# All eight gate/up k tiles in rounded and remainder parts, with a GpSimd subtraction, and four raw down-weight buffers

## What is computed

```python
def _swiglu(x, wg, wu, wd):
    return (jax.nn.silu(x @ wg) * (x @ wu)) @ wd

def run_block(args):
    xblk, e = args
    return _swiglu(xblk, w_gate[e], w_up[e], w_down[e])

yb = lax.map(run_block, (xb, block_e)).reshape(p, d)
yb = yb * buf_w[:, None].astype(yb.dtype)
return jax.ops.segment_sum(yb, buf_tok, num_segments=n + 1)[:n]
```

## Time and profile before

| | us |
|---|---|
| median of 3 runs | 1226.64 (1225.98 to 1227.47) |
| the profiled execution | 1225.67 |
| its span, first to last instruction | 1223.5 |
| PE busy | 1106.1 (90%) |
| DVE busy | 903.4 (74%) |
| ACT busy | 642.7 (53%) |
| POOL busy | 181.9 (15%) |

### The profile page before, as it was taken

The page is one execution under the profiler, slowest core; times in us unless marked ns, Lnnn a source line. Parts: engine busy times, 40 slices in busy tenths (PEclk is TensorE's granted clock), DMA queues, the critical chain, the costliest instruction groups (busy, mean ns, idle before and its releaser), DMA issues.

```text
span 1223.5 us, 18540 instructions
## 1 busy us (share of the span) xinstructions
PE 1106.1 (90%) x6014; PEld 811.6 (66%) x6014; DVE 903.4 (74%) x1333; ACT 642.7 (53%) x770; POOL 181.9 (15%) x185
## 2 busy tenths in 40 slices
PE   5999999999989999799999999999999999999700
PEld 3899999865444454467777777777777777777500
DVE  4422443365956777579899999989989888888878
ACT  4332221332421233257787777777777777777501
POOL 1000000000110110112222222222222222221102
PEclk9999999998879999899999999999999999999855
DMA  9542221436974143689999999999999999998996
GB/s 341 188 133 80 80 80 40 157 98 202 315 276 132 44 138 120 235 325 381 380 388 391 391 384 385 387 387 381 373 381 383 373 381 379 375 375 314 352 360 210
DMA packets 86545, 339.34 MB, mean 277 GB/s; under 512 B 12561, under 2 KB 36129, under 8 KB 59122
## 3 DMA queue, kind: packets, MB, share of 16 engines
q1 hardware_dynamic: 70130, 301.16, 67.2%
q0 software_dynamic: 16384, 37.78, 8.8%
HBM read 317.00 MB, written 42.86 MB: 294 GB/s over the span
## 4 chain that ended last, share of the span: by engine, by line
PE 46%; DMA 32%; DVE 14%; ACT 6%; issue 2%; SPq 1%; DVEq 0%; POOL 0%; POOLq 0%; ACTq 0%
DMA arena<-in_w_exp_down 28%; PE ps L1828 11%; DVE down_lo L1648 4%; PE ps L2259 4%; PE ps L2067 4%; ACT down_hi L1120 4%; PE ps L2238 3%; PE ps L2239 3%; PE ps L2240 3%; PE ps L1821 2%; PE ps L2242 1%; PE ps L2105 1%; PE ps L2226 1%; DMA arena<-expert_rows 1%; PE ps L2140 1%
## 5 line engine op out<-in xcount | busy, mean ns | idle before, releaser
L1653 DVE TENSOR_TENSOR gu_lo<-w_gu,gu_hi 128x2048 fp32r<-128x2048 f32 (+1 forms) x128 | 258.7, 2022 | 6.4 <-ACT gu_hi L1114 1.1
L1114 ACT ACTIVATE gu_hi<-w_gu 128x2048 fp32r<-128x2048 f32 (+1 forms) x128 | 217.9, 1703 | 0.0
L1648 DVE TENSOR_TENSOR down_lo<-arena,down_hi 128x2048 fp32r<-128x2048 f32 x64 | 146.7, 2293 | 58.0 <-ACT down_hi L1120 58.0
L2238 PE MATMUL ps<-gu_hi,xT_hi 128*112 128x512 f32 x448 | 182.8, 408 | 3.3 <-DVE xT_lo L1658 2.2
L2239 PE MATMUL ps<-gu_lo,xT_hi 128*112 128x512 f32 x448 | 177.9, 397 | 0.0
L2240 PE MATMUL ps<-gu_hi,xT_lo 128*112 128x512 f32 x448 | 177.3, 396 | 0.0
L1120 ACT ACTIVATE down_hi<-arena 128x2048 fp32r<-128x2048 f32 x64 | 122.7, 1918 | 64.0 <-DMA arena<-in_w_exp_down 56.1
L814 POOL DMA_INDIRECT expert_rows<-arena,row_idx x64 | 69.1, 1079 | 356.2 <-ACT arena L1159 340.1
L2259 PE MATMUL ps<-down_hi,actT_hi 128*112 128x512 f32 x256 | 106.6, 416 | 5.5 <-DVE actT_lo L1643 5.5
L807 POOL DMA_INDIRECT arena<-h_rows,token_idx x64 | 80.6, 1259 | 203.1 <-PE ps L2226 156.1
L1828 PE MATMUL ps<-w_hi,hT_hi 128*128 128x300 f32 x352 | 105.6, 300 | 1.4 <-DVE w_lo L1231 1.4
(11 more groups left out here) (310 smaller groups left out, 1989.8 us busy)
## 6 DMA issues: line engine op xcount, KB each, us to landing
w_gu<-in_w_exp_gate SPq DMA_DIRECT2D x64, 1024.0 KB
w_gu<-in_w_exp_up SPq DMA_DIRECT2D x64, 1024.0 KB
arena<-in_w_exp_down SPq DMA_DIRECT2D x64, 1024.0 KB
arena<-in_w_ada SPq DMA_DIRECT2D x16, 1024.0 KB, 6.9
arena<-in_w_in SPq DMA_DIRECT2D x12, 1200.0 KB, 5.6
arena<-expert_rows SPq DMA_DIRECT2D x9, 1024.0 KB, 13.4
arena<-in_w_ada_first SPq DMA_DIRECT2D x4, 2048.0 KB, 16.2
arena<-expert_rows SPq DMA_DIRECT2D x4, 2048.0 KB, 13.0
```

The costliest lines, as they stand in the source:

```text
L1114: a.activation(gu_hi[b % RING][:, :, ks], w_gu[b % U][:, :, ks], ACT.Copy).then_inc(s_ghi, 1)
L1648: v.tensor_tensor(down_lo[:, :, :], w_dn[b % RING], down_hi[:, :, :].bitcast(F32), ALU.subtract).then_inc(s_dlo, 1)
L1653: v.tensor_tensor(gu_lo[b % U][:, :, ks], w_gu[b % U][:, :, ks], gu_hi[b % RING][:, :, ks].bitcast(F32), ALU.subtract).then_inc(s_glo, 1)
L2238: pe.matmul(out, x_hi, gu_hi[r][:, :, k], start=(k == 0), stop=False)
```

## The change

All eight k tiles get rounded and remainder parts (SPLIT = 8), so the plain float32 product, `x_raw` and its ACT copy are gone. ACT's second part of `gu_hi` and `xT_hi`, and DVE's `xT_lo`, grow by one k tile; DVE's `gu_lo` stays at seven tiles (LOW_PARTS), and the eighth is subtracted by POOL (`last_k_low`). There are four raw down buffers; two of them lie in two separate pieces of 1024 columns each. SP fills buffers 2 and 3 before the loop and then loads the down weights of block j+4, not j+2. Nine small loads of modulation rows (`bcg2`) move from ahead of the loop to the end, and three other regions move to make room.

```diff
-SPLIT = 7
+SPLIT = 8
 PARTS = ((0, 4), (4, SPLIT))
+LOW_PARTS = ((0, 4), (4, SPLIT - 1))
...
-        w_dn = [region(a + W_COLS[0], FK, D) for a in RING_AT]
+        w_dn = [region(a + W_COLS[0], FK, D) for a in RING_AT] + [apart(PROJ0 + 4 * D, PROJ0 + 9 * D), apart(*DN3)]
...
                 if wait:
-                    sp.wait_ge(s_dlo, j - RING + 1)
+                    sp.wait_ge(s_dlo, j - U + 1)
...
             load_gate_up(3, 3, False)
-            sp.dma_start(bcg2[0].rearrange("p (c n) -> p c n", n=512), mod_row[1, 0:1, 2:4].broadcast_to([P, 2, 512])).then_inc(s_bcg, 16)
-            for b in range(SB):
-                sp.dma_start(bcg2[1][b * SS:(b + 1) * SS].rearrange("p (c n) -> p c n", n=512),
-                             mod_row[1, 1 + b:2 + b, 2:4].broadcast_to([SS, 2, 512])).then_inc(s_bcg, 16)
+            load_down(2, 2, False)
+            load_down(3, 3, False)
...
                     load_gate_up(i * U + (U + b), b, True)
-                    load_down(i * U + (b + RING), (b + RING) % U, True)
+                    load_down(i * U + (U + b), b, True)
...
+            def last_k_low(j, b):
+                g.wait_ge(s_ghi, j * 2 + 2)
+                g.tensor_tensor(gu_lo[b % U][:, :, SPLIT - 1], w_gu[b % U][:, :, SPLIT - 1], gu_hi[b % RING][:, :, SPLIT - 1].bitcast(F32),
+                                ALU.subtract).then_inc(s_gat, 1)
...
                         gather(i * U + (b + GATHER_AHEAD), (b + GATHER_AHEAD) % U)
+                    if not is_last or b + 2 < U:
+                        last_k_low(i * U + (b + 2), b + 2)
...
-                a.activation(x_raw[:, b % 2], xT_ps[:, SPLIT:KT], ACT.Copy).then_inc(s_xth, 1)
...
                     for k in range(*PARTS[part]):
+                        if k == SPLIT - 1:
+                            pe.wait_ge(s_gat, j + 2)
...
-                        pe.matmul(out, x_lo, gu_hi[r][:, :, k], start=False, stop=False)
-                for k in range(SPLIT, KT):
-                    o = pe.matmul(out, x_raw[:, b % 2, k - SPLIT], w_gu[q][:, :, k], start=False, stop=(k == KT - 1))
+                        o = pe.matmul(out, x_lo, gu_hi[r][:, :, k], start=False, stop=(k == KT - 1))
```

More of the change, by code:

```diff
@@ L106 @@
 W_COLS = (2 * KT * FF, FK * D)
+GU_HI0, GU_HI1 = WORK0 + W_COLS[0] + W_COLS[1], HT0 + D // 2
+assert GU_HI0 + 2 * KT * FF == WORK0 + 10 * D and GU_HI1 + 2 * KT * FF <= ST0
 def _constants():
@@ L202, in hybrid_step @@
         actT_lo = over_arena("actT_lo", MOD0 + 2 * FK * D + 2 * FK * T, [P, 2, FK, T])
[L203 removed]
+        gu_hi = [over_arena(f"gu_hi{n}", at, [P, 2, SPLIT, FF]) for n, at in enumerate((GU_HI0, GU_HI1))]
         gu_lo = [over_arena(f"gu_lo{n}", at, [P, 2, KT, FF]) for n, at in enumerate(GU_AT)]
@@ L332, in hybrid_step, with apart @@
         rowf = small(5, P, rows=1)
-        tab = region(_consts["before"][0] + P, 4, P, rows=1).bitcast(I32)
+        tab = region(TAB0, 4, P, rows=1).bitcast(I32)
         act_rows = region(MOD0 + 2 * FK * D + 4 * FK * T, 2, FF)
         silu_g = region(MOD0 + 2 * FK * D + 4 * FK * T + 2 * FF, 2, FF)
-        w_dn = [region(a + W_COLS[0], FK, D) for a in RING_AT]
+        def apart(first, second):
+            return arena[:, first:first + 2 * (second - first)].rearrange("p (k n) -> p k n", k=FK)[:, :, 0:D]
+        DN3 = (ARENA_W - 2 * (ARENA_W - WORK0 - 10 * D), WORK0 + 10 * D)
+        w_dn = [region(a + W_COLS[0], FK, D) for a in RING_AT] + [apart(PROJ0 + 4 * D, PROJ0 + 9 * D), apart(*DN3)]
+        assert DN3[0] >= HB0 + 2 * D and DN3[0] + D <= WORK0 and DN3[1] + D == GU_HI1
         x_rows = region(HB0, 2, D)
@@ L469, in hybrid_step @@
         s_wgu = [sem(f"w_gate_up_in{b}") for b in range(U)]
-        s_wdn = [sem(f"w_down_in{r}") for r in range(RING)]
+        s_wdn = [sem(f"w_down_in{r}") for r in range(RING)] + [s_cond, s_const]
+        WDN_BASE = (0, 0, 32, 32)
         s_dhi = sem("w_down_high_ready")
@@ L734, in _ @@
                 rank_rows(ranks_low[t], 0, 4, t)
-            load_down(last * U + 3, 3, True)
             for t in range(2, NT):
@@ L741, in _ @@
                 rank_rows(ranks_low[t], 0, 4, t)
+                if t == 2:
+                    for b in range(SB):
+                        sp.dma_start(bcg2[1][b * SS:(b + 1) * SS].rearrange("p (c n) -> p c n", n=512),
+                                     mod_row[1, 1 + b:2 + b, 2:4].broadcast_to([SS, 2, 512])).then_inc(s_bcg, 16)
             sp.wait_ge(s_gu, last * U + 4)
+            sp.wait_ge(s_dlo, last * U + 3)
             for rows, buf in kept(N, shared):
@@ L745, in _ @@
             sp.wait_ge(s_free, last * U + 4)
-            sp.wait_ge(s_dlo, last * U + 3)
             for t in LAST_ORDER:
@@ L823, in _ @@
             g.wait_ge(s_tab, 1)
-            for j in range(GATHER_AHEAD):
-                gather(j, j, j >= 2)
+            for j in range(2):
+                gather(j, j, False)
+            last_k_low(0, 0)
+            gather(2, 2)
+            gather(3, 3)
+            last_k_low(1, 1)
             def turn(i, is_last, is_first=False):
```

42 lines of the change are left out of this document (20 added, 22 removed).

## The result

The changed kernel takes 1237.9 us in the median of six runs (1233.4 to 1240.5), the kernel before 1226.3 us in six runs beside it. The ratio is 1.0101, 95% interval 1.0077 to 1.0125. The forecast was 1227 us and a range up to 1234 us. That execution is the slowest of the six: these two lie 14.9 us apart, the medians 11.6.

What follows compares the result with a forecast made beforehand. PE and DMA were taken as full together, DVE close behind. 62 x (9.88 - 9.86) = 1.2 us longer and 0.9 us shorter put 1225.67 at 1226.0 us, plus 1.0 us to the median: 1227 us, range 1214 to 1234 us.

Steps and rivals of the forecast that it cites:

- The end: After the loop: one 1.05 MB load leaves, 0.79 MB in nine small loads comes in between rank rows, costing zero.
- PE, 0.15 us a step shorter: Loop, PE: the 0.86 us float32 product goes, three single-pass products (0.71 us) come; step 9.63 us, 9.3 us over 62 steps.
- Four down buffers give back 4.8 us: Loop: down loads get two more steps, so the wait for late down loads goes, worth 4.8 us if the data comes.
- ACT and `xT_lo` cost nothing: Loop: ACT ends about 0.4 us later ahead of a waiting `down_hi`; DVE's `xT_lo` grows 0.14 us, hidden by idle time.
- DVE's reserve of 0.84 us: Loop: DVE's idle time per block in the kernel before, said to hide the longer `xT_lo`.
- GpSimd's subtraction, t = 1.15 us, and the two hold each other up: Loop: POOL's eighth-tile subtraction takes t, 1.15 us, and it and DVE's `gu_lo` delay each other by that whole length.
- 9.30 + t/2: Loop: lower bound in us on one step from the two-step ACT and DVE chain, t being POOL's subtraction time; 9.88 us.
- The step of 9.88 us, loop 603 us: Loop: forecast step against 9.86 us before; silu of block 1 to silu of block 62 takes 603 us.
- main case: Whole kernel: POOL and DVE hold each other up, PE waits for `xT_lo`; 1227 us, chance 0.48.
- Rival 1: Loop: POOL and DVE run side by side, DMA gives back 5.7 of 14.1 us; gain 9.3 us, 1217 us; chance 0.27.
- 0.9 us gained at `down_hi` of block 63: Last block: with its down load there before, `down_hi` waits only for PE and 0.9 us is gained.
- The signs: Expected in the profile: float32 product and `down_hi` load waits gone, PE waiting for `xT_lo`, `gu_lo` longer or later, step 9.88 us.

Runs made afterwards that it cites:

- e1: Changed kernel without its eight small loads of sample modulation rows in the end (sample rows get a wrong gate row): end 76.2 us, against 90.9.
- e12: Changed kernel with the eight loads replaced in place by one 0.5 MB load of the prompt's row, 128 partitions, 2 KB packets: ratio 1.0098 to the kernel before.
- e13: Changed kernel with the eight loads replaced in place by one 0.5 MB load of different DRAM rows, 2 KB packets: end 86.8 us, ratio 1.0063.
- e14: Changed kernel with the eight loads replaced in place by one 0.5 MB load of 128 whole rows, 4 KB packets: end 83.3 us, ratio 1.0056.
- e15: Changed kernel with one more SyncE wait: the fourth read of `expert_rows` is issued only once the eight loads have landed; end 81.2 us.
- e6: Changed kernel with down loads inside the loop cut to one of two k tiles (wrong outputs): loop 614.8 us, end 76.3 us.
- e7: Kernel of e2 with down loads inside the loop cut to one of two k tiles: loop 594.6 us.
- e3: Changed kernel with two raw down buffers instead of four, both late down loads back in the end: loop 602.7 us, end 90.4 us.
- e11: Kernel before, with the eight sample-row loads issued again between the third and fourth read of `expert_rows`: median 1236.5 us, slower by 0.96%.
- e2: Changed kernel without GpSimd's subtraction and PE's wait for it, PE reading the rounded last k tile instead: loop 604.6 us, first ten steps 9.64 us.
- e4: Changed kernel with the eighth k tile's remainder also made by VectorE, GpSimd doing none: loop 601.1 us, first ten steps 9.61 us.
- e9: Changed kernel with the eight sample-row loads issued behind the last read of `expert_rows`: time equal to the kernel before.
- e5: Changed kernel with the same sample rows at the same place brought by two loads of 64 partitions instead of eight: end 89.4 us.
- e10: Changed kernel with the load placing of e9 and the all-VectorE remainders of e4: 0.2% below the kernel before, interval to 1.0001.
- e8: Kernel before with down loads inside the loop cut to one of two k tiles: loop 601.0 us, against 601.4.

## Why the prediction was wrong, step by step

**The failed step is "The end": the 0.79 MB in nine small loads "issued between rank rows that are not yet due: zero".** The end is 13.7 us longer than before, and without the eight loads 14.7 us shorter than that (90.9 and 76.2, e1). The step counted bytes and due times. But a load is there only when its last part is, and the parts can drift apart.

What the runs show: wherever the fifth read had a spread of 1.0 us or less, the end took 75.6 to 81.2 us; wherever it had 3.3 us or more, 83.3 to 90.9 us, in 17 traces without exception. Where the fourth read had come with a spread of 4.1 us or less, the fifth was in step again; from 4.6 us on it never was, nor any later read. The fifth is issued only after an addition, about when the fourth lands, which gives laggards a pause to catch up in: from 1158 to 1160 us the DMA share is 0.62 in e1, and 1.03 in the changed kernel. That this is how step is regained is argued from these traces, and e15 shows that a pause does it. The loop hands over engines that are 0.6 to 4.6 us apart (third read), and one more load between the third and the fourth read, whichever it is (e12 to e14), takes them past what the pause can mend.

That lost step makes packets slow is shown as far as two things go. In e15 one wait is added, nothing less is moved, and the spread and the slow packets are both gone; but the wait also leaves fewer loads in the queue at once. In e6 and e7 the end's list of loads is that of the changed kernel, the eight included, the reads stay in step, and packets take 190 ns. Why packets take longer when the parts are out of step was not tried.

Why e6 and e7 kept in step isn't tested either. Their third reads had spreads of 0.7 and 1.0 us, but so had those of e3 and e11 (0.8, 1.0), which lost it. What differs is the queue: in e6 and e7 the fourth read was issued only 1.6 and 2.7 us before the last part of the third landed, in the changed kernel, e3 and e11 6.5 to 6.9 us before. So it stood in a queue that had nearly run dry, which fits e15.

**PE, 0.15 us a step shorter.** Right: the first ten steps of e2 are 9.64 us for 9.63 predicted.

**Four down buffers give back 4.8 us.** Wrong, it is nothing (e3). `down_hi`'s wait for loads did go; since the step was set by DVE's chain and by the transfers, it was worth nothing. The prediction read the late steps of before (9.96 us in the last 21) as the price of two buffers, but with four they are the same, 9.96.

**ACT and `xT_lo` cost nothing.** ACT: right. DVE's reserve of 0.84 us is used up by the subtraction.

**GpSimd's subtraction, t = 1.15 us, and the two hold each other up.** Right in kind: t is 1.27 and 1.29 us in the rows above, and `gu_lo` is longer by what it had to wait; where DVE goes first, `down_low` is held up in its place, as foretold. The rule of the Trainium skill (SBUF — State Buffer, "Who interferes with whom") that the two exclude each other agrees with the trace, except that the wait shows inside the later instruction's row. PE waits for `xT_lo` as foretold, 0.18 us in the block shown and 2.9 us in the 30 blocks from 700 to 1000 us. By 9.30 + t/2 the step would be 9.94 us; it is 9.84 in the unbroken stretches and 602.5/61 = 9.88 over the loop. The formula lets `gu_lo` begin t later; in the rows it is delayed by 0.84 and 1.06 us only, the rest of POOL's operation having passed before DVE is ready. Half of that on 9.30 us gives 9.72 to 9.83 us.

**The step of 9.88 us, loop 603 us.** It is 602.5 us, but half of this is luck. The prediction took DMA as full and not as a bound in its main case. e2 and e4 have no hold-up and gain nothing: the transfers stand at the same pace. Two bounds lay on each other, 9.84 us from the engines and 9.85 to 9.91 from the transfers (601.1 and 604.6 us by 61), and the prediction named one. Rival 1 (side by side, DMA gives back 5.7 of 14.1 us) undersized it as well: DMA gives back everything.

**0.9 us gained at `down_hi` of block 63.** Right, but small beside the rest: `down_hi` starts when PE is done, at 1150.43 us, and the additions begin 7.6 us behind silu of block 63, before 8.3 us: 0.7 us gained.

**The signs.** Those of the loop came as written. None was given for the end, since nothing was expected to happen there.

## What to carry to other kernels

A load moved into a stretch where the queue is never empty is not costed by its bytes: look at where the queue runs dry now, because that is where the DMA engines fall back into step, and put what is not urgent behind the last urgent read (e9) or wait for it (e15). GB/s well under its usual value at a full DMA share is the sign. And where two resources are full in the same window, don't credit a gain to relieving one: without the hold-up alone (e2, e4) or with fewer bytes alone (e6) the loop was no more than 1.4 us shorter, and only both together (e7) made it 8 us shorter.

## What the runs showed of the hardware

- The median 4 KB packet of before's whole trace took 159 ns. In the end the mean was 187 to 193 ns with the reads in step and 194 to 235 ns out of step, at the same DMA share: 14 to 17% of the packets took over 250 ns in step, 18 to 31% out of step.
- Even in step, the stretch in which the 64-row tile is read runs at about half speed (197 to 233 GB/s in e1 from 1160 to 1165 us, where 414 to 426 stand before and behind). The fifth read, 1 MB for 64 partitions, landed 4.9 us behind the fourth, which is 2 MB for 128 partitions and landed 6.2 us behind the third (last parts).
- One of the 16 parts of a load lags far behind the others in the loop: from 700 to 1000 us the spread of a down load is 14 to 17 us (median) in the changed kernel, e1, e2, e4, e5, e9, e10 and e12 to e15, which have four down buffers, 8 to 10 us in before, e3 and e11, which have two, and 1 us in e6 to e8, whose loads are cut. With deeper buffers the other parts run further ahead of the last one, and a load still counts from its last part; that would explain why depth gave no time, but no run tests it.
- A DVE subtraction that finds GpSimd's subtraction at work on the same buffers shows no idle time; it is longer in its own row. The group means of `gu_lo` (2332 ns for 2027) and `down_low` (2546 for 2293) show it, waits don't. GpSimd's row grows likewise when it is the second (2.96 us for 1.27), so its mean of 1780 ns is not its working time.
- Fewer bytes made a loop slower: e6 took 12 us more than the changed kernel, with "issue" time ahead of `act`. Why is open.
